# The relative bias of a banded attention: from reversing products on TensorE to a reversed key order and an add on VectorE

## The chip, the cores and the metric

One Trainium2 chip, one of its cores. The metric is the device time of one execution in microseconds (us). Lower is better. All matrices are float32; in the large projections each operand is split into two float32r parts (high and low), in the two attentions plain float32 products are used.

## The reference, cut to what matters

The reference is one transformer block with two attentions and 32 experts, and then two more blocks. Only the second attention of the first block is touched. It has 8 heads of 64, a sequence of 256, and a relative position bias:

```
q = q * 64**-0.5                                 # 8 heads, 256 positions, 64 columns
rel  = (kj - pad_len) - qi                       # key position less query position
bias = rel_bias[:, clip(rel, -128, 128) + 128]   # (8 heads, queries, keys)
s = einsum('bhqd,bhkd->bhqk', q, k) + bias
p = softmax(where(valid, s, -inf))               # whole chunks of 64 keys: not later than the query's chunk
o = einsum('bhqk,bhkd->bhqd', p, v)
```

With 256 positions no key lies further back than the band reaches, so the mask only hides the chunks of 64 keys that come after the query's own. The softmax is over all keys, so the order in which the keys stand in a row of scores does not matter to the sum and the maximum; the product with v needs them in the order of v.

## The kernel before, in words

The program is a sequence of phases. Each is a block in which the five engines run their own instruction lists and meet at its end. The first three are `phase_in`, `phase_attend` and `phase_merge`; then come the experts and the second block's phases.

`phase_in` projects the normed input into ten panels of 512 columns. SP loads weight chunks of 1 MB into a ring of four slots `raw`, ScalarE makes the high part `wh` (L156), VectorE the low part `wl` (L162), TensorE multiplies (L175 and L191), VectorE copies each finished panel out of PSUM (L489 to L497). Panels 3 and 4 are the queries and the keys of the second attention, `qkb`. Meanwhile GpSimd makes the tables: `ident`, then `rel_wide` (the bias of each head over 512 relative distances, clipped ends filled in), which it stores to DRAM as `rel_rows`. From there it loads `rel` by eight skewed transfers, one for each head (L430): partition p of a head gets the 384 numbers that start at p. It also makes `flip` (a 128x128 matrix with ones on the counter-diagonal), `mask` (0 or -1e30) and `alibi` (the first attention's bias with the mask added, L449 and L450).

In such a skewed table a row runs the wrong way: with the partition taken as the query, distance grows with the partition, while it should fall. The kernel puts that right by a product: `flip` (the counter-diagonal) turns the order of the partitions round, and the product is accumulated onto the scores in the same PSUM bank (L595).

`phase_attend` works through 16 units. A unit is one pair of heads (second attention) or one head with its two maps (first attention), and one tile of 128 queries. Units 0 to 7 are the first attention, 8 to 15 the second. TensorE's list in iteration u is written out by hand:

```
scores(u + 1)      # L592, two products of 64 rows; from unit 8 on each is followed by one of L595
mod_chunk(...)     # L301, one chunk of ada_w of the second block, 1 MB, straight from raw
mix(u - 2)         # L618 or L622, weights times v
flip(u - 1)        # L605, transposes of the weights
```

In iterations 0 to 3 a second `mod_chunk` follows. `scores(u)` waits for `biased` of unit u-2, `mix` for `keyed` and `kept`, `flip` for `weighed`. VectorE's list in iteration u is `bias(u)` (L707: scores plus `alibi` or `mask`, then the row maximum L710), `weigh(u - 1)` (L718 to L725: reciprocal of the row sum and the scaling of the weights `a`) and `keep(u - 2)` (L731). ScalarE does `exps(u)` (L656) and `key(u - 1)` (L665: the transposed weights out of PSUM). SP loads the `ada_w` chunks into the four slots of `raw` as `mod_chunk` frees them.

After the last unit VectorE normalises the first attention's output, TensorE transposes all of it, and the phase ends. `phase_merge` then multiplies with the branch weights and `w_out`, routes the tokens, and its SP list issues the first loads of expert weights, into buffers that lie over those of the attention. The experts' stage follows.

Of the kernel before, what the change touches and what calls it, by code (L numbers as in the profile page):

```python
# [14 lines left out]
P = 128  # L15
# [15 lines left out]
HB = 8  # L31
# [35 lines left out]
def make_mixing(c, ctx):  # L67

    c.qkb = c.sb("qkb", [P, 2, 4, S], ctx=ctx)
    c.va = c.sb("va", [P, TT, 512], ctx=ctx)  # L70
    c.vb = c.sb("vb", [P, TT, 512], ctx=ctx)
    c.mask = c.sb("mask", [P, TT, S], ctx=ctx)
    c.alibi = c.sb("alibi", [P, HA, TT, S], ctx=ctx)
    c.rel = c.sb("rel", [P, HB, 384], ctx=ctx)


def make_experts(c):


    with ExitStack() as early:  # L80
        make_mixing(c, early)
    left = c.sb("moe_left", [P, 2, BIG_CHUNK], ctx=c.moe)
    c.choice = c.sb("choice", [P, TT, 2, CAP], ctx=c.moe)
    c.slot_number = c.sb("slot_number", [P, SLOTS], ctx=c.moe)
    c.bias_in = c.sb("bias_in", [P, E * 16], ctx=c.moe)
    c.back = c.sb("back", [P, S], ctx=c.moe)
    make_routing(c)
    with ExitStack() as early:
        make_split(c, "1", early)
    halves = c.sb("moe_halves", [P, RING, BIG_CHUNK], ctx=c.moe)  # L90
    whole = c.raw[:, :, :, :].rearrange("p (s r) k n -> p s (r k n)", r=2)
    c.moe_ring = Stream(c, "moe_", [left[:, s] for s in range(2)] + [halves[:, s] for s in range(RING)]
                        + [whole[:, s] for s in range(RING // 2)])
    c.items = Items(c)
# [260 lines left out]
def phase_in(c):  # L355
# [4 lines left out]
    w_in = d["w_in"][0]  # L360
    c.qka = c.sb("qka", [P, 2, 4, S], ctx=c.mix)
    c.gates = c.sb("gates", [P, TT, 2 * D], ctx=c.mix)
    c.flip = c.sb("flip", [P, P], ctx=c.mix)
    c.at = c.sb("at", [P, 2, 512], ctx=c.mix)
    c.lam_in = c.at[:, 0, 0:4 * DA].rearrange("p (i j n) -> p i j n", i=2, j=2)
    c.subln = c.sb("subln", [P, 128], ctx=c.mix)
# [17 lines left out]
    with ExitStack() as local, nc.Block() as block:  # L384
        gain = c.sb("ln_in_gain", [P, D], ctx=local)
        shift = c.sb("ln_in_shift", [P, D], ctx=local)
        rel_wide = c.sb("rel_wide", [HB, 512], ctx=local)
        dist = c.sb("dist", [P, TT, S], ctx=local)
        away = c.sb("away", [P, TT, S], ctx=local)

# [16 lines left out]
        @block.gpsimd  # L407
        def _(pool):
            pool.memset(c.ident[:, :], 0.0).then_inc(ident_step, 1)
            pool.wait_ge(ident_step, 1)  # L410
            pool.affine_select(out=c.ident[:, :], in_=c.ident[:, :], compare_op=ALU.not_equal, fill=1.0, base=0,
                               pattern=[[-1, P]], channel_multiplier=1).then_inc(ident_step, 1)
            steps = 0

            def done(ins):
                nonlocal steps
                steps += 1
                ins.then_inc(pool_step, 1)
                pool.wait_ge(pool_step, steps)

            pool.wait_ge(bias_loaded, 16)
            lo, hi = S - 1 - CLIP, S - 1 + CLIP
            pool.tensor_copy(rel_wide[:, 0:lo], rel_wide[:, lo:lo + 1].to_broadcast([HB, lo]))
            done(pool.tensor_copy(rel_wide[:, hi + 1:512], rel_wide[:, hi:hi + 1].to_broadcast([HB, 511 - hi])))
            pool.dma_start(rel_rows, rel_wide[:, :]).then_inc(rel_stored, 16)
            pool.wait_ge(rel_stored, 16)
            for h in range(HB):
                pool.dma_start(c.rel[:, h, :], bass.AP(tensor=rel_rows.tensor, offset=h * 512, ap=[[1, P], [1, 384]])  # L430
                               ).then_inc(c.rel_loaded, 16)
            done(pool.memset(c.flip[:, :], 0.0))
            done(pool.affine_select(out=c.flip[:, :], in_=c.flip[:, :], compare_op=ALU.not_equal, fill=1.0,
                                    base=1 - P, pattern=[[1, P]], channel_multiplier=1))
            done(pool.memset(c.mask[:, :, :], 0.0))
            for m in range(TT):
                done(pool.memset(c.mask[0:CHUNK, m, m * P + CHUNK:S], NEG))
                if m < TT - 1:
                    done(pool.memset(c.mask[CHUNK:P, m, m * P + P:S], NEG))
            done(pool.iota(dist[:, :, :], pattern=[[P, TT], [-1, S]], base=0, channel_multiplier=1,  # L440
                           allow_small_or_imprecise_dtypes=True))
            done(pool.tensor_scalar(away[:, :, :], dist[:, :, :], -1.0, None, ALU.mult))

            for t, sign in ((dist, 1), (away, -1)):
                done(pool.affine_select(out=t[:, :, :], in_=t[:, :, :], compare_op=ALU.is_ge, fill=0.0, base=0,
                                        pattern=[[sign * P, TT], [-sign, S]], channel_multiplier=sign))
            done(pool.tensor_tensor(dist[:, :, :], dist[:, :, :], away[:, :, :], ALU.add))
            for h in range(HA):
                done(pool.tensor_scalar(away[:, :, :], dist[:, :, :], -2.0 ** (-8.0 * (h + 1) / HA), None, ALU.mult))  # L449
                done(pool.tensor_tensor(c.alibi[:, h], away[:, :, :], c.mask[:, :, :], ALU.add))  # L450
            pool.sem_inc(c.bias_ready, 1)

        @block.scalar
# [16 lines left out]
        @block.vector  # L470
        def _(dve):
            dve.wait_ge(x_loaded, 16 * TT)
            dve.wait_ge(norm_loaded, 32)
            layer_norm_dve(c, dve, 0, c.x, gain[:, :], shift[:, :])
            dve.sem_inc(normed, 1)
            for n in range(AHEAD):
                split_low(c, dve, W + n, n)
            turn_dve(c, dve, 0, c.bank)
            for p in range(panels):
                for n in range(2 * p + AHEAD, min(2 * p + AHEAD + 2, after)):  # L480
                    split_low(c, dve, W + n, n % RING)
                dve.wait_ge(c.used, W + 2 * p + 2)
                banks = c.bank[p % 2 * 2:p % 2 * 2 + 2]
                if p == 6:
                    dve.wait_ge(gate_loaded, 16)
                for b in range(2):
                    if kinds[p] == "T":

                        last = dve.tensor_scalar(outs[p][:, 2 * b:2 * b + 2, :],  # L489
                                                 banks[b][:, :].rearrange("p (k s) -> p k s", k=2),  # L490
                                                 SCALE if p in (0, 3) else 1.0, None, ALU.mult)
                    elif p < 6:
                        last = dve.tensor_copy(outs[p][:, b, :], banks[b][:, :])
                    else:
                        g = slice((p - 6) * COLS, (p - 5) * COLS)

                        last = dve.tensor_tensor(c.gates[:, b, g], banks[b][:, :], c.gates[:, TT - 1, g], ALU.add)  # L497
                        if b < TT - 1:
                            linked(c, dve, last)
                last.then_inc(evacuated, 1)  # L500
            dve.sem_inc(gates_ready, 1)
# [22 lines left out]
def phase_attend(c):  # L524
# [23 lines left out]
    with ExitStack() as local, nc.Block() as block:  # L548
# [34 lines left out]
        def _(pe):  # L583
            def scores(u):
# [4 lines left out]
                for j in range(2):  # L589
                    half = slice(j * 64, j * 64 + 64)  # L590
                    out = c.bank[2 * (u % 2) + j][:, 0:S]
                    mm = pe.matmul(out, qk[half, 0, h, m * P:m * P + P], qk[half, 1, h, :],  # L592
                                   start=True, stop=u < diff)
                    if u >= diff:
                        mm = pe.matmul(out, c.flip[:, :], c.rel[:, 2 * h + j, P - m * P:P - m * P + S],  # L595
                                       start=False, stop=True)
                mm.then_inc(scored, 1)

            def flip(u):
# [26 lines left out]
            scores(0)  # L626
            pe.wait_ge(silu_step, 2)
            for u in range(units + 2):
                if u + 1 == diff:
                    pe.wait_ge(c.rel_loaded, 16 * HB)  # L630
                if u + 1 < units:
                    scores(u + 1)
                mod_chunk(c, pe, part, u + min(u, EXTRA))
# [52 lines left out]
        def _(dve):  # L686
# [14 lines left out]
            def bias(u):  # L701
                h, m = u % diff // 2, u % 2
                dve.wait_ge(scored, u + 1)
                if u >= 2:
                    dve.wait_ge(weighed, u - 1)
                b = c.alibi[:, h, m] if u < diff else c.mask[:, m]
                dve.tensor_tensor(s[:, u % 2], c.psum[:, 2 * (u % 2):2 * (u % 2) + 2, 0:S],  # L707
                                  b.unsqueeze(1).to_broadcast([P, 2, S]), ALU.add).then_inc(biased, 1)
                dve.wait_ge(biased, u + 1)
                dve.tensor_reduce(nmax[:, u % 2, :], s[:, u % 2], AX, ALU.max, negate=True).then_inc(maxed, 1)  # L710

            def weigh(u):
# [9 lines left out]
                    dve.scalar_tensor_tensor(a[:, u % 2, 0], e[:, u % 2, 0], share[:, 0:1], a[:, u % 2, 1],  # L722
                                             ALU.mult, ALU.add).then_inc(weighed, 1)
                else:
                    dve.tensor_tensor(a[:, u % 2], e[:, u % 2], share[:, :].unsqueeze(2).to_broadcast([P, 2, S]),  # L725
                                      ALU.mult).then_inc(weighed, 1)

            def keep(u):
# [539 lines left out]
def phase_experts(c):  # L1268
# [9 lines left out]
    c.hid = c.sb("hid", [P, 2, COLS], ctx=c.exp)  # L1278
    c.y = c.sb("y", [P, COLS], ctx=c.exp)
    c.weighed = c.sb("weighed", [P, TT, SLOTS], ctx=c.exp)  # L1280
    c.acts = c.sb("acts", [P, KT, CAP], ctx=c.exp)
    c.gate_half = c.sb("gate_half", [P, 8, CAP], ctx=c.exp)
    c.up_half = c.sb("up_half", [P, 8, CAP], ctx=c.exp)
    c.sig = c.sb("sig", [P, 8, CAP], ctx=c.exp)
# [1264 lines left out]
```

## Time and profile before

| | us |
|---|---|
| median of 3 runs | 2092.8 (2089.57 to 2092.97) |
| profiled execution, its own time | 2093.78 |
| span of the profiled execution | 2092.0 |
| PE busy | 1839.9 (88%) |
| DVE busy | 788.3 (38%) |
| ACT busy | 489.4 (23%) |
| POOL busy | 50.0 (2%) |
| mean granted clock of TensorE | 0.945 of full |

The span is the time between the first and the last instruction that the profiler recorded. PE is TensorE's matmul, DVE is VectorE, ACT is ScalarE, POOL is GpSimd, SP is the engine that issues most loads. A float32 product appears as two matmul records. Durations of single matmuls overlap (they are pipelined), so that the work of a stretch of TensorE is read from the distance between starts, not from the sum of durations. The same holds, to a smaller degree, for VectorE. The second attention's units lie between about 176 and 220 us of the span.

### The profile page before, as it was taken

To read this page: it belongs to the slowest core of one execution; us is meant where nothing else is said; L and a number is where in the kernel's file an instruction comes from. 1 tells how busy PE (TensorE), PEld (TensorE's weight loads), DVE (VectorE), ACT (ScalarE), POOL (GpSimd) and SP (SyncE) were. 2 spreads that over 40 slices of the span, in tenths; PEclk is the share of its full clock that TensorE was granted. 3 is DMA by queue.
4 is the path that set the end of the run, shared out by engine and by line. 5 is a ranking of instruction groups with operands and counts; after the bars stand their busy time and mean duration, and the time that the engine had idled before them with its cause. 6 is when DMAs were issued, how large, how long until landed. Compare 5 with 4: busy or idle time off the path is not lost. (4 is left out here: it accounts for less than half of the span.)

```text
span 2092.0 us, 23989 instructions
## 1 busy us (share of the span) xinstructions
PE 1839.9 (88%) x9794; PEld 1132.5 (54%) x9795; DVE 788.3 (38%) x1024; ACT 489.4 (23%) x557; POOL 50.0 (2%) x74
## 2 busy tenths in 40 slices
PE   5999678999999898999999982978799979987998
PEld 5864454333333333333333321957688856566887
DVE  5545552221211221112211215556555555355544
ACT  3323421010100101010100002323243333234342
POOL 5000000000000000000000001010000000000000
PEclk9999888999999999999999996998899989788999
DMA  7548468999999999999999986544455523663651
GB/s 282 178 146 313 164 264 363 427 428 427 429 428 428 429 428 429 428 428 428 429 428 429 426 336 210 191 145 143 141 173 200 200 92 137 207 228 118 206 192 59
DMA packets 130798, 603.47 MB, mean 288 GB/s; under 512 B 12752, under 2 KB 12888, under 8 KB 106032
## 3 DMA queue, kind: packets, MB, share of 16 engines
q1 hardware_dynamic: 120096, 587.23, 70.9%
q10 hardware_dynamic: 10096, 13.77, 2.0%
q0 software_dynamic: 544, 1.59, 0.2%
q8 instruction: 45, 0.74, 0.1%
q14 instruction: 17, 0.14, 0.0%
HBM read 601.45 MB, written 1.11 MB: 288 GB/s over the span
## 5 line engine op out<-in xcount | busy, mean ns | idle before, releaser
L162 DVE TENSOR_TENSOR wl<-raw,wh 128x2048 fp32r<-128x2048 f32 x126 | 285.2, 2301 | 94.0 <-ACT wh L156 84.6
L156 ACT ACTIVATE wh<-raw 128x2048 fp32r<-128x2048 f32 x126 | 236.5, 1908 | 210.6 <-PE banks L175 124.8
L1156 PE MATMUL banks<-moe_halves,xs 128*64 128x512 f32 x1024 | 233.0, 603 | 12.0 <-DMA moe_halves<-in_w_exp_in 12.0
L191 PE MATMUL banks<-xth,wh 128*128 128x256 f32 x800 | 228.2, 285 | 11.0 <-DVE xtl L252 11.0
L191 PE MATMUL banks<-xtl,wh 128*128 128x256 f32 x800 | 228.2, 285 | 0.0
L191 PE MATMUL banks<-xth,wl 128*128 128x256 f32 x800 | 228.2, 285 | 0.0
L1205 DVE COPY hid<-banks 128x512 f32<-128x512 f32 x32 | 22.1, 692 | 523.0 <-PE banks L1156 523.0
L191 PEld LDWEIGHTS banks<-xth,wh 128*128 128x128 f32 x800 | 154.2, 193 | 12.9 <-DVE xtl L252 12.6
L1156 PEld LDWEIGHTS banks<-moe_halves,xs 128*64 128x64 f32 x1024 | 70.9, 138 | 159.8 <-issue 127.5
L175 PE MATMUL banks<-wh,xth 128*128 128x512 f32 x352 | 143.8, 409 | 13.3 <-PEq L548 5.9
L191 PEld LDWEIGHTS banks<-xtl,wh 128*128 128x128 f32 x800 | 153.3, 192 | 0.3
L191 PEld LDWEIGHTS banks<-xth,wl 128*128 128x128 f32 x800 | 153.0, 191 | 0.0
L175 PE MATMUL banks<-wl,xth 128*128 128x512 f32 x352 | 142.5, 405 | 0.0
L175 PE MATMUL banks<-wh,xtl 128*128 128x512 f32 x352 | 142.3, 404 | 0.0
L1156 PE MATMUL banks<-moe_left,xs 128*64 128x512 f32 x544 | 122.5, 597 | 6.0 <-DMA moe_left<-in_w_exp_in 5.9
L1168 PE MATMUL banks<-moe_halves,acts 128*64 128x512 f32 x512 | 114.7, 597 | 10.6 <-DMA moe_halves<-in_w_exp_out 10.6
L1156 PE MATMUL banks<-raw,xs 128*64 128x512 f32 x480 | 107.9, 596 | 4.5 <-DMA raw<-in_w_exp_in 4.5
L175 PE MATMUL banks<-wh,act_l 128*128 128x512 f32 x256 | 101.3, 396 | 0.0
L175 PE MATMUL banks<-wl,act_h 128*128 128x512 f32 x256 | 101.3, 396 | 0.0
L175 PE MATMUL banks<-wh,act_h 128*128 128x512 f32 x256 | 101.3, 396 | 0.0
L175 PEld LDWEIGHTS banks<-wh,xth 128*128 128x128 f32 x352 | 68.5, 195 | 32.3 <-issue 10.4
L1156 PEld LDWEIGHTS banks<-moe_left,xs 128*64 128x64 f32 x544 | 37.1, 137 | 83.2 <-issue 64.1
(342 smaller groups left out, 2052.1 us busy)
## 6 DMA issues: line engine op xcount, KB each, us to landing
moe_halves<-in_w_exp_in SPq DMA_DIRECT2D x64, 2048.0 KB, 34.7
moe_left<-in_w_exp_in SPq DMA_DIRECT2D x34, 2048.0 KB, 33.5
moe_halves<-in_w_exp_out SPq DMA_DIRECT2D x32, 2048.0 KB, 31.1
raw<-in_mlp_w SPq DMA_DIRECT2D x64, 1024.0 KB, 5.6
raw<-in_w_exp_in SPq DMA_DIRECT2D x30, 2048.0 KB, 34.7
raw<-in_ada_w SPq DMA_DIRECT2D x48, 1024.0 KB, 6.0
raw<-in_w_exp_out SPq DMA_DIRECT2D x18, 2048.0 KB, 31.1
moe_left<-in_w_exp_out SPq DMA_DIRECT2D x14, 2048.0 KB, 33.9
```

The lines of the kernel that those rows point to most:

```text
L156: act.activation(c.wh[:, slot], c.raw[:, slot], ACT.Copy).then_inc(c.high_ready, 1)
L162: dve.tensor_tensor(c.wl[:, slot], c.raw[:, slot], c.wh[:, slot].bitcast(F32), ALU.subtract).then_inc(c.low_ready, 1)
L175: mm = pe.matmul(banks[m][:, :], x[:, k0 + k, toks], w[:, slot, k], start=first and k == 0 and j == 0, stop=last and k == CK - 1 and j == ...
L191: mm = pe.matmul(out, w[:, slot, k, cols], x[:, k0 + k, :], start=first and k == 0 and j == 0 and b % 2 == 0, stop=last and k == CK - 1 an ...
L1156: mm = pe.matmul(c.bank[hid_banks(c, par) + pn][half * HALF:half * HALF + HALF, :], c.xs[:, 2 * k + r, own * CAP:own * CAP + CAP], st.slot ...
L1168: mm = pe.matmul(c.bank[hid_banks(c, par)][half * HALF:half * HALF + HALF, :], c.acts[:, 4 * j + r, :], st.slots[slot][:, at:at + COLS], s ...
L1205: dve.tensor_copy(c.hid[:, 1, :], c.bank[hid_banks(c, par) + 1]).then_inc(it.up_kept, 1)
```

## The change

The bias is laid out so that no turning is needed in TensorE. The stored rows are reversed (`rel_back`), and each head gets two skewed transfers of 256 numbers, one for each tile of queries, instead of one of 384. Along a row of the table the keys now run backwards. So the keys of the second attention are stored backwards too, by the copy out of PSUM of panel 4; the scores come out with reversed keys; and when VectorE scales the weights, it writes them with a negative step, so that they are in the usual order again for the transposes and the product with v. The mask, reversed, is added into `rel` by GpSimd, once. VectorE's add of unit 8 and later takes `rel` where it took `mask`. `flip` and the products L595 are gone. TensorE's wait for `rel_loaded` before unit 8 becomes a wait of VectorE for `bias_ready` at 2. `mask` lives in `phase_in` alone; `rel` grows from 384 to 512 numbers for each head; `acts` is allocated earlier, so that the tiles laid over the attention's buffers still cover them.

```diff
-    c.mask = c.sb("mask", [P, TT, S], ctx=ctx)
-    c.rel = c.sb("rel", [P, HB, 384], ctx=ctx)
+    c.rel = c.sb("rel", [P, HB, TT, S], ctx=ctx)
@@ make_experts / phase_experts
+    c.acts = c.sb("acts", [P, KT, CAP], ctx=c.moe)
-    c.acts = c.sb("acts", [P, KT, CAP], ctx=c.exp)
@@ phase_in, gpsimd
-            pool.dma_start(rel_rows, rel_wide[:, :]).then_inc(rel_stored, 16)
+            done(pool.tensor_copy(rel_back[:, 0:511], rel_wide[:, 510::-1]))
+            pool.dma_start(rel_rows[:, 0:511], rel_back[:, 0:511]).then_inc(rel_stored, 16)
             pool.wait_ge(rel_stored, 16)
             for h in range(HB):
-                pool.dma_start(c.rel[:, h, :], bass.AP(tensor=rel_rows.tensor, offset=h * 512, ap=[[1, P], [1, 384]])
-                               ).then_inc(c.rel_loaded, 16)
-            done(pool.memset(c.flip[:, :], 0.0))
-            done(pool.affine_select(out=c.flip[:, :], in_=c.flip[:, :], compare_op=ALU.not_equal, fill=1.0,
-                                    base=1 - P, pattern=[[1, P]], channel_multiplier=1))
+                for m in range(TT):
+                    pool.dma_start(c.rel[:, h, m, :], bass.AP(tensor=rel_rows.tensor, offset=h * 512 + m * P,
+                                                              ap=[[1, P], [1, S]])).then_inc(c.rel_loaded, 16)
...
             pool.sem_inc(c.bias_ready, 1)
+            pool.wait_ge(c.rel_loaded, 16 * HB * TT)
+            for h in range(HB):
+                done(pool.tensor_tensor(c.rel[:, h], c.rel[:, h], mask[:, :, ::-1], ALU.add))
+            pool.sem_inc(c.bias_ready, 1)
@@ phase_in, vector
-                        last = dve.tensor_scalar(outs[p][:, 2 * b:2 * b + 2, :],
+                        out = outs[p][:, 2 * b:2 * b + 2, ::-1] if p == 4 else outs[p][:, 2 * b:2 * b + 2, :]
+                        last = dve.tensor_scalar(out,
@@ phase_attend, tensor
                     mm = pe.matmul(out, qk[half, 0, h, m * P:m * P + P], qk[half, 1, h, :],
-                                   start=True, stop=u < diff)
-                    if u >= diff:
-                        mm = pe.matmul(out, c.flip[:, :], c.rel[:, 2 * h + j, P - m * P:P - m * P + S],
-                                       start=False, stop=True)
+                                   start=True, stop=True)
...
-                if u + 1 == diff:
-                    pe.wait_ge(c.rel_loaded, 16 * HB)
@@ phase_attend, vector
-                b = c.alibi[:, h, m] if u < diff else c.mask[:, m]
-                dve.tensor_tensor(s[:, u % 2], c.psum[:, 2 * (u % 2):2 * (u % 2) + 2, 0:S],
-                                  b.unsqueeze(1).to_broadcast([P, 2, S]), ALU.add).then_inc(biased, 1)
+                if u == diff:
+                    dve.wait_ge(c.bias_ready, 2)
+                b = (c.alibi[:, h, m].unsqueeze(1).to_broadcast([P, 2, S]) if u < diff
+                     else c.rel[:, 2 * h:2 * h + 2, m])
+                dve.tensor_tensor(s[:, u % 2], c.psum[:, 2 * (u % 2):2 * (u % 2) + 2, 0:S], b, ALU.add
+                                  ).then_inc(biased, 1)
...
-                    dve.tensor_tensor(a[:, u % 2], e[:, u % 2], share[:, :].unsqueeze(2).to_broadcast([P, 2, S]),
+                    dve.tensor_tensor(a[:, u % 2, :, ::-1], e[:, u % 2], share[:, :].unsqueeze(2).to_broadcast([P, 2, S]),
                                       ALU.mult).then_inc(weighed, 1)
```

## Rows read from the trace of the kernel before

**Rows 1.** Page: busy tenths of PE and of the DMA engines in 40 slices.

```profile
PE   5999678999999898999999982978799979987998
...
DMA  7548468999999999999999986544455523663651
```

**Rows 2.** Busy by stretch: stretch, length, PE, PEld, DVE, ACT, POOL, granted clock, DMA share, GB/s.

```profile
149.00:153.00 4.00, 4.00 (x20) 0.86 (x20) 3.46 (x10) 1.64 (x7) 0.00 (x0) 0.50 0.17 25
160.00:170.00 10.00, 7.13 (x52) 2.63 (x52) 3.74 (x12) 2.57 (x9) 0.00 (x0) 1.00 1.05 392
176.00:214.00 38.00, 38.00 (x208) 19.45 (x208) 19.09 (x45) 12.84 (x40) 0.00 (x0) 1.00 0.75 264
...
360.00:1200.00 840.00, 785.65 (x3824) 305.28 (x3820) 160.69 (x338) 88.14 (x145) 0.00 (x0) 1.00 1.01 428
```

**Rows 3.** Timeline of PE, one unit of the second attention: start, length, what.

```profile
204.13 0.69 PE L592 MATMUL banks<-qkb 64*128 64x256 f32 x2
204.76 0.70 PE L595 MATMUL banks<-rel,flip 128*128 128x256 f32 x2
...
206.64 1.07 PE L301 MATMUL banks<-raw,silu_c 128*32 128x512 f32 x8
207.64 1.11 PE L622 MATMUL banks<-vb,at 128*128 128x64 f32 x8
208.58 0.61 PE L605 MATMUL banks<-ident,a 128*128 128x128 f32 x4
209.12 0.70 PE L592 MATMUL banks<-qkb 64*128 64x256 f32 x2
```

**Rows 4.** Timeline of PE, first attention, and the second's first and last start.

```profile
148.01 1.23 PE L592 MATMUL banks<-qka 64*128 64x256 f32 x4 [2.05 <-DVE silu_c L689]
149.16 3.64 PE L301 MATMUL banks<-raw,silu_c 128*32 128x512 f32 x16
...
162.78 1.07 PE L301 MATMUL banks<-raw,silu_c 128*32 128x512 f32 x8 [1.01 <-DMA raw<-in_ada_w]
...
173.15 0.70 PE L592 MATMUL banks<-qka 64*128 64x256 f32 x4
173.78 1.06 PE L301 MATMUL banks<-raw,silu_c 128*32 128x512 f32 x8
...
175.86 0.70 PE L592 MATMUL banks<-qkb 64*128 64x256 f32 x2
...
214.11 1.06 PE L301 MATMUL banks<-raw,silu_c 128*32 128x512 f32 x8
```

**Rows 5.** Timeline of DVE, one iteration in the second attention.

```profile
208.78 0.29 DVE L731 COPY o<-banks 128x128 f32<-128x128 f32 x1 [2.58 <-PE banks L622]
208.99 0.68 DVE L707 TENSOR_TENSOR s<-banks,mask 128x512 f32<-128x512 f32 x1
209.71 0.69 DVE L710 TENSOR_REDUCE nmax<-s 128x2 f32<-128x512 f32 x1
210.31 0.15 DVE L718 RECIPROCAL share<-total 128x2 f32<-128x2 f32 x1
210.50 0.69 DVE L725 TENSOR_TENSOR a<-s,share 128x512 f32<-128x512 f32 x1
```

**Rows 6.** Timeline of POOL in the first phase.

```profile
22.10 4.28 POOL L430 DMA_DIRECT2D rel<-rel_rows  x8 [6.91 <-DMA rel_rows<-rel_wide]
...
43.24 1.31 POOL L450 TENSOR_TENSOR alibi<-away,mask 128x512 f32<-128x512 f32 x1
...
48.14 2.35 POOL L450 TENSOR_TENSOR alibi<-away,mask 128x512 f32<-128x512 f32 x1
```

**Rows 7.** Timeline of DVE in the first phase.

```profile
43.60 5.72 DVE L162 TENSOR_TENSOR wl<-raw,wh 128x2048 fp32r<-128x2048 f32 x2
...
54.91 4.48 DVE L162 TENSOR_TENSOR wl<-raw,wh 128x2048 fp32r<-128x2048 f32 x2
64.90 1.29 DVE L493 COPY va<-banks 128x512 f32<-128x512 f32 x2 [5.51 <-PE banks L175]
```

More of the change, by code:

```diff
@@ L362, in phase_in @@
     c.gates = c.sb("gates", [P, TT, 2 * D], ctx=c.mix)
-    c.flip = c.sb("flip", [P, P], ctx=c.mix)
     c.at = c.sb("at", [P, 2, 512], ctx=c.mix)
@@ L386, in phase_in @@
         shift = c.sb("ln_in_shift", [P, D], ctx=local)
-        rel_wide = c.sb("rel_wide", [HB, 512], ctx=local)
+        mask = c.sb("mask", [P, TT, S], ctx=local)
+        rel_wide = c.at[0:HB, 1, :]
+        rel_back = c.sb("rel_back", [HB, 512], ctx=local)
         dist = c.sb("dist", [P, TT, S], ctx=local)
@@ L426, in _ @@
             done(pool.tensor_copy(rel_wide[:, hi + 1:512], rel_wide[:, hi:hi + 1].to_broadcast([HB, 511 - hi])))
-            pool.dma_start(rel_rows, rel_wide[:, :]).then_inc(rel_stored, 16)
+            done(pool.tensor_copy(rel_back[:, 0:511], rel_wide[:, 510::-1]))
+            pool.dma_start(rel_rows[:, 0:511], rel_back[:, 0:511]).then_inc(rel_stored, 16)
             pool.wait_ge(rel_stored, 16)
             for h in range(HB):
-                pool.dma_start(c.rel[:, h, :], bass.AP(tensor=rel_rows.tensor, offset=h * 512, ap=[[1, P], [1, 384]])
-                               ).then_inc(c.rel_loaded, 16)
-            done(pool.memset(c.flip[:, :], 0.0))
-            done(pool.affine_select(out=c.flip[:, :], in_=c.flip[:, :], compare_op=ALU.not_equal, fill=1.0,
-                                    base=1 - P, pattern=[[1, P]], channel_multiplier=1))
-            done(pool.memset(c.mask[:, :, :], 0.0))
+                for m in range(TT):
+                    pool.dma_start(c.rel[:, h, m, :], bass.AP(tensor=rel_rows.tensor, offset=h * 512 + m * P,
+                                                              ap=[[1, P], [1, S]])).then_inc(c.rel_loaded, 16)
+            done(pool.memset(mask[:, :, :], 0.0))
             for m in range(TT):
-                done(pool.memset(c.mask[0:CHUNK, m, m * P + CHUNK:S], NEG))
+                done(pool.memset(mask[0:CHUNK, m, m * P + CHUNK:S], NEG))
                 if m < TT - 1:
-                    done(pool.memset(c.mask[CHUNK:P, m, m * P + P:S], NEG))
+                    done(pool.memset(mask[CHUNK:P, m, m * P + P:S], NEG))
             done(pool.iota(dist[:, :, :], pattern=[[P, TT], [-1, S]], base=0, channel_multiplier=1,
@@ L449, in _ @@
                 done(pool.tensor_scalar(away[:, :, :], dist[:, :, :], -2.0 ** (-8.0 * (h + 1) / HA), None, ALU.mult))
-                done(pool.tensor_tensor(c.alibi[:, h], away[:, :, :], c.mask[:, :, :], ALU.add))
+                done(pool.tensor_tensor(c.alibi[:, h], away[:, :, :], mask[:, :, :], ALU.add))
+            pool.sem_inc(c.bias_ready, 1)
+            pool.wait_ge(c.rel_loaded, 16 * HB * TT)
+            for h in range(HB):
+                done(pool.tensor_tensor(c.rel[:, h], c.rel[:, h], mask[:, :, ::-1], ALU.add))
             pool.sem_inc(c.bias_ready, 1)
```

## The prediction

> **What bounds the kernel now.** I read the page first. TensorE is busy in 9 tenths of most slices, and in the middle of the span the DMA engines are too [rows 1]. The busy time by stretch then says which stage has which limit. Between 360 and 1200 us, the experts, the DMA share is 1.01 at 428 GB/s [rows 2]: that stage goes at the pace of the loads. The changed stretch, 176 to 214 us, is another sort: TensorE is busy in all of its 38.00 us at a granted clock of 1.00, VectorE in 19.09, ScalarE in 12.84, and the loads use 0.75 of the DMA engines [rows 2]. There TensorE's own list is the limit.
>
> The timeline of TensorE shows the list without a gap: one unit of the second attention takes from 204.13 to 209.12, which is 4.99 us [rows 3]. It splits, by starts, into 206.64 - 204.13 = 2.51 us of scores and bias products, 1.00 of the ada_w chunk, 0.94 of `mix` and 0.54 of transposes. VectorE waits 2.58 us for `mix` in each of these units [rows 5]. So what TensorE loses from its list comes off the unit, until another chain is the slowest.
>
> Does a gain at 214 us reach the end? What follows (the last units, the norm, the transposes, the merge) is a chain that starts with the last unit's weights; the experts' loads are issued by SP inside the merge, behind its barrier and its products. So the load-bound stage starts earlier by what the attention saves, and nothing in it has a start of its own. I take the shift to be carried whole.
>
> **The products that go.** Each unit has two pairs of records of L595. By the starts the first takes 204.76 to about 205.39, and the four pairs of L592 and L595 together take the 2.51 us: 0.63 each [rows 3]. Removing two pairs gives 1.26 us for each unit, eight units: 10.0 us.
>
> **What the removed products kept apart.** This is the term that the diff does not show. The two score products of a unit use 64 rows each, one the lower half of the array's rows, the other the upper. In the first attention they follow each other directly, and all four records together take 173.15 to 173.78, 0.63 us [rows 4]. In the second attention, with a product of 128 rows between them, two records alone take 0.63 us [rows 3]. Same shapes, same clock (1.00), half the time for each. So next to each other the halves run at the same time, and apart they don't. After the change they stand next to each other in the second attention too: another 0.63 us for each unit. The scores fall from 2.51 to 0.63, by 1.88 us. The Trainium skill, TensorEngine Tiling (Array Packing), Key Properties, says that tiles of the array work independently and that a change of the tiling mode drains the array; the trace agrees, with 0.63 us for four records against 0.63 us for two.
>
> **The unit after.** TensorE: 4.99 - 1.88 = 3.11 us. Is anything else slower? VectorE: its iteration takes, by starts, 0.72 (L707), 0.60 (L710), 0.19 (L718), 0.69 (L725) and 0.21 (L731), that is 2.41 us [rows 5]. The chain across engines: `keep` and so the whole iteration of VectorE starts when `mix` ends (208.78, at 209.12 - 0.34), and the weights are ready at 211.19, 2.07 us after the unit's start. `flip` needs them at 0.63 + 1.00 + 0.94 = 2.57 us after the start. Slack 0.50 us. ScalarE has 12.84 us of work in 38.00, about 1.7 for each unit of 4.99 [rows 2], and fits in 3.11 with room. The chunk loads: at 392 GB/s a chunk of 1.049 MB takes 2.68 us, and at that pace the first attention already waits for them (1.01 us before the chunk at 162.78) [rows 2, 4]. A unit of 3.11 us is above 2.68, though by little.
>
> The first units of the stretch are different, because `mix` and the transposes are still those of the first attention. From 175.86 to 214.11 there are eight iterations, 38.25 us [rows 4]; five at 4.99 are 24.95, so the first three are 13.30, 4.43 each. Less 1.88 that is 2.55 us, under the pace of the loads of 2.68. I put 2.7 for each.
>
> Sum: 38.25 before, 3 x 2.7 + 5 x 3.11 = 23.65 after, 14.6 us less. After 214.11 no scores are left, and the tail is as it was.
>
> **VectorE's operands.** The add L707 has the same size, with `rel` in place of a broadcast `mask`: 0.68 us as before; the alibi and the mask form have that shape. The scaling L725 writes with a step of minus one. No row shows such a write. Below: no gain is possible from an order, so 0.69 us. Above: twice that, 1.38 us, by which VectorE would be at half its rate. I take 0.69, since the engine goes one element after another (512 numbers in 0.69 us) and the order only changes the address. At 1.38 the weights come at 2.76 against 2.57: `flip` is late by 0.19 us and more through the chain's next turn, 0.1 to 0.3 for a unit, and 0.7 for the last one, in which nothing hides it: about 2 us in all, a saving of 12.6. The copy of panel 4 writes backwards too; before the copy of a panel VectorE sits idle 5.51 us [rows 7], so even twice 1.29 us is hidden.
>
> **GpSimd's work.** It gains one reversed copy over 8 partitions, eight more transfers to issue (4.28 us for eight [rows 6]) and eight adds of 128x512, each 1.31 to 2.35 us, as the alibi adds [rows 6]; it loses the two operations on `flip`. The alibi adds now end at 48.14 + 2.35 = 50.5 us; afterwards at 50.5 + 4.3 plus a little, and the eight adds 10.5 to 18.8 us later: 65 to 75 us. They are first wanted at about 178 us: over 100 us of cover. The transfers bring 16 x 128 rows of 1 KB, 2.10 MB, instead of 8 x 128 rows of 1.5 KB, 1.57 MB; at 392 GB/s [rows 2] the difference is 1.3 us of the DMA engines, and a ring of four chunks covers that for the projections. Cost: nothing. Without that cover it would be VectorE's unit 8 that waits, and TensorE behind it.
>
> What the adds may disturb is VectorE's splitting. It did before: two splits took 5.72 us while GpSimd worked on the tables, and 4.48 us when it did not [rows 7]. That is 1.24 us of a reserve of 5.51 for each panel; 15 to 25 us of new GpSimd work touch two or three panels. Even a delay of 4.5 us, a doubling, would be hidden. The Trainium skill, SBUF — State Buffer, Who interferes with whom, says that a VectorE instruction with two SBUF inputs contends with a GpSimd instruction that reads SBUF, and that the second to issue waits for the whole of the other; the trace agrees with a loss (1.24 us), and by that rule too the sum stays as it is.
>
> **The sum against the run.** The profiled execution took 2093.78 with a span of 2092.0. Span after: 2092.0 - 14.6 = 2077.4, its time 2079.2. The median before was 2092.8, 1 us under the profiled one: predicted median 2078.2, 0.70% less. No change that a measurement of this kernel can tell is one within 0.2%, 4.2 us.
>
> **Rivals.**
>
> A, the forecast: 14.6 us, 2078.2. Chance 0.70.
>
> B, only the reversing products' own time goes: the score halves stay one after the other for a reason of the second attention's own. 10.0 us, 2082.8. For it: the halves of `qkb` have never been seen next to each other. Against: the forms of the records are the same as of `qka`, and the 0.63 us for four records holds there. 0.09.
>
> C, VectorE becomes the slowest: the negative step costs up to double. 12.6 us, 2080.2; with the add slower too, less. For: slack of only 0.50 us. Against: nothing in the rows; it is unknown rather than indicated. 0.11.
>
> D, the other side: TensorE's clock falls in the second attention, because its list is no longer gapless. At the lower of the two levels (granted 0.50 between 149 and 153 us, 1.2 GHz against 2.4) the four records of L592 took 148.01 to 149.16, 1.15 us, instead of 0.63: 1.83 times [rows 2, 4]. Then five units of 3.11 x 1.83 = 5.7 and three of 4.7 make 42.6 us, 4.3 over the present 38.25, and the last units' 2.5 us grow by 2: slower by 6.3, 2099.1. It decides from the point where over two thirds of the stretch is at the lower level. Against: between 160 and 170 us TensorE is busy 7.13 of 10 us, with gaps of 1 us, and is granted 1.00 [rows 2]; the new stretch is nearly gapless. 0.03.
>
> E, the change does not do what it says in time: `rel` with the mask is late at unit 8. It would need to be ready only after 178 us to cost anything, and after 193 us to eat all; with 65 to 75 us that takes adds of 14 us each instead of 1.31 to 2.35. Time 2092.8 at 193 us. 0.01.
>
> F, the gain is given back later: a stage after the attention has a limit of its own, or the clock rises later after the pauses of the tail. Nothing in the rows has such a start; a rest for the unknown. Within 4.2 us of before: about 2090. 0.06.
>
> **How the numbers follow.** A alone: the three first units may take 2.5 to 3.1 and the others 3.1 to 3.3, and medians before spread over 3.4 us, so 2075.0 to 2081.5. B and C add the upper part: range 2074.8 to 2084.0, which leaves D, E, F and half of the tails out. Faster by over 0.2%: A, B, C, 0.90, and a little of F, 0.91. Same 0.05, slower 0.04.
>
> **What the profile after should show.** In the second attention four records of L592 in 0.63 us, directly followed by L301; no row of L595 (its number shifts) with `flip`; starts of units 3.1 us apart; VectorE idle before `keep` 0.7 us instead of 2.58; L725 at 0.69 us; DMA share near 0.9 to 1.0 in the stretch; `phase_merge` starting at 227 instead of 241.6 us; the experts' stage of the same length. Two records in 0.63 us would show B; L725 over 0.69 us C; a granted clock under 1.00 between 176 and 205 us D. I would be wrong above all if the halves don't overlap, or if the chunk loads, at 2.68 us a piece, are slower there.

## The result

| | kernel before | changed kernel |
|---|---|---|
| median | 2092.39 us (6 runs) | 2075.59 us (6 runs) |
| profiled execution, its own time | 2093.78 | 2076.02 |
| span | 2092.0 | 2074.2 |

The ratio of the two is 0.9912, with a 95% interval of 0.9887 to 0.9937: 18.4 us faster, where 14.6 was forecast. The ratio applied to the first median, 2092.8, gives 2074.4, just under the range's low end of 2074.8. The direction, the place and the mechanism in the attention held; a term was missing, and it lies 1000 us after the place of the change.

One execution weighs on this ratio. Five of the six of the changed kernel took 2074.38 to 2077.65 us, the sixth 2062.65, and it alone has a mean granted clock of 0.955 where the five have 0.942 to 0.946. Without it the averages are 2092.23 and 2076.01 us, a ratio of 0.9922 and 16.2 us, which is 2076.6 on the first median and inside the range. The last experiments below show what such an execution may be.

The timeline of TensorE in the changed kernel shows the stretch that the forecast was about, with its first three iterations, one later unit and the end:

```profile
175.68 0.70 PE L598 MATMUL banks<-qkb 64*128 64x256 f32 x4
176.31 1.06 PE L301 MATMUL banks<-raw,silu_c 128*32 128x512 f32 x8
...
178.56 0.70 PE L598 MATMUL banks<-qkb 64*128 64x256 f32 x4
...
181.26 0.70 PE L598 MATMUL banks<-qkb 64*128 64x256 f32 x4
183.12 1.06 PE L301 MATMUL banks<-raw,silu_c 128*32 128x512 f32 x8 [1.15 <-DMA raw<-in_ada_w]
...
194.52 0.70 PE L598 MATMUL banks<-qkb 64*128 64x256 f32 x4
195.15 1.07 PE L301 MATMUL banks<-raw,silu_c 128*32 128x512 f32 x8
196.14 1.10 PE L625 MATMUL banks<-vb,at 128*128 128x64 f32 x8
197.09 0.61 PE L608 MATMUL banks<-ident,a 128*128 128x128 f32 x4
197.62 0.70 PE L598 MATMUL banks<-qkb 64*128 64x256 f32 x4
...
200.73 1.06 PE L301 MATMUL banks<-raw,silu_c 128*32 128x512 f32 x8
```

All four score records of a unit now fit in 0.63 us (175.68 to 176.31), as in the first attention [rows 4], and a unit takes 3.10 us (194.52 to 197.62) instead of 4.99 [rows 3]. The stretch from 175.68 to 200.73 takes 25.05 us instead of 38.25 [rows 4]: 13.2 us less.

VectorE's timeline in the same unit answers to [rows 5]:

```profile
194.18 0.29 DVE L735 COPY o<-banks 128x128 f32<-128x128 f32 x1 [0.70 <-PE banks L625]
194.39 0.68 DVE L711 TENSOR_TENSOR s<-banks,rel 128x512 f32<-128x512 f32 x1
195.10 0.69 DVE L714 TENSOR_REDUCE nmax<-s 128x2 f32<-128x512 f32 x1
195.71 0.15 DVE L722 RECIPROCAL share<-total 128x2 f32<-128x2 f32 x1
195.90 0.69 DVE L729 TENSOR_TENSOR a<-s,share 128x512 f32<-128x512 f32 x1
```

The write with a negative step takes 0.69 us, the same as forwards; the wait for `mix` fell from 2.58 to 0.70.

Busy time by stretch in the changed kernel (columns as in [rows 2]):

```profile
176.00:201.00 25.00, 23.67 (x180) 12.44 (x180) 19.18 (x45) 12.82 (x41) 0.00 (x0) 1.00 1.05 386
...
360.00:1200.00 840.00, 785.91 (x3822) 306.11 (x3820) 162.57 (x338) 88.50 (x145) 0.00 (x0) 0.99 1.01 428
```

The granted clock stayed at 1.00, so rival D did not come. But the DMA share in the attention is now 1.05: the loads are as full there as TensorE.

GpSimd and VectorE in the first phase, where the tables are made:

```profile
21.93 8.49 POOL L434 DMA_DIRECT2D rel<-rel_rows  x16 [6.17 <-DMA rel_rows<-rel_back]
...
51.68 14.90 POOL L455 TENSOR_TENSOR rel<-rel,mask 128x512 f32<-128x512 f32 x8 [0.18 <-POOL alibi L451]
```

```profile
54.39 5.57 DVE L162 TENSOR_TENSOR wl<-raw,wh 128x2048 fp32r<-128x2048 f32 x2
64.39 1.29 DVE L499 COPY va<-banks 128x512 f32<-128x512 f32 x2 [4.42 <-PE banks L175]
```

The adds end at 66.6 us, 110 us before they are wanted. While they run VectorE loses 1.1 us in a panel (5.57 against 4.48) and its idle time falls from 5.51 to 4.42 [rows 7]: hidden, as forecast.

**Where the rest came from.** Subtracting the times of the same events in the two traces gives the gain as it stood at each:

| event | before | after | difference |
|---|---|---|---|
| first scores of the second attention | 175.86 | 175.68 | -0.2 |
| first chunk product after the last scores | 214.11 | 200.73 | -13.4 |
| first product of the merge | 241.62 | 228.60 | -13.0 |
| first load issued in the experts' phase | 336.96 | 322.71 | -14.3 |
| last product of the experts | 1254.73 | 1240.56 | -14.2 |
| VectorE's first instruction of the next phase | 1264.94 | 1244.81 | -20.1 |
| start of the norm behind it | 1271.70 | 1253.76 | -17.9 |
| span | 2092.0 | 2074.2 | -17.8 |

The attention's gain is carried through the load-bound stage. The 1.3 us that come on top in the merge go with the granted clock: between its first product and the first load of the experts' phase it is 0.85 on average before and 0.90 after, and TensorE is busy 77.1 against 75.6 us for the same 350 matmuls. From 28 to 38 us into the merge the clock is 0.50 before, and 0.72 and then 1.00 after.

Then 6.0 us more appear between two instructions, of which 2.2 are given back at the next wait. Here is that place in both kernels, before and after, first TensorE's last product of the experts and then VectorE:

```profile
1254.73 1.99 PE L1191 MATMUL banks<-y,back 64*128 64x512 f32 x8 [0.69 <-ACT y L1216]
```

```profile
1264.94 2.35 DVE L1593 SCALAR_TENSOR_TENSOR x<-x,banks 128x1024 f32<-128x1024 f32 x2 [20.61 <-PEq L1454]
1271.70 2.47 DVE L215 BATCH_NORM_STATS2 stats<-x 128x6 f32<-128x512 f32 x4 [4.40 <-DMA ln<-in_ln_b]
```

```profile
1240.56 1.99 PE L1195 MATMUL banks<-y,back 64*128 64x512 f32 x8 [0.69 <-ACT y L1220]
```

```profile
1244.81 2.35 DVE L1596 SCALAR_TENSOR_TENSOR x<-x,banks 128x1024 f32<-128x1024 f32 x2 [14.51 <-PEq L1457]
1253.76 2.47 DVE L215 BATCH_NORM_STATS2 stats<-x 128x6 f32<-128x512 f32 x4 [6.60 <-DMA ln<-in_ln_b]
```

This is the dead time: from the end of the product to VectorE's start it is 8.22 us before (1256.72 to 1264.94) and 2.26 us after (1242.55 to 1244.81). No engine does anything in between. What lies there in the program is `phase_spill`: code for tokens over an expert's capacity, a long body of TensorE's instructions, that is skipped by a branch when there are none. The releaser that the row names is TensorE's sequencer (PEq) at that phase.

### The profile page after: what moved, and what is told of

Read it like the earlier page. It is cut to its first block and busy times, and to the rows that moved or that the text cites. A ratio compares the mean times of both kernels' runs of the same rounds, so it can differ in the third digit from the quotient of the medians.

```text
span 2074.2 us, 23939 instructions
## 1 busy us (share of the span) xinstructions
PE 1827.8 (88%) x9762; PEld 1124.7 (54%) x9763; DVE 789.5 (38%) x1024; ACT 489.5 (24%) x557; POOL 66.1 (3%) x89
## 5 line engine op out<-in xcount | busy, mean ns | idle before, releaser
L175 PE MATMUL banks<-wh,xth 128*128 128x512 f32 x352 | 143.2, 407 | 14.3 <-PEq L554 5.9
```

Of the source, the lines that this page charges most:

```text
L175: mm = pe.matmul(banks[m][:, :], x[:, k0 + k, toks], w[:, slot, k], start=first and k == 0 and j == 0, stop=last and k == CK - 1 and j == ...
```

## The experiments

**The place of the code behind the skip.** The change takes 32 matmul and 32 weight-load instructions out of TensorE's program, and a wait. Everything behind moves forward in the program by that much. Two kernels put that to the test, one in each direction, by waits on a count that has long been reached. The expectations reckon 130 waits as 64 instructions and 382 as 192, and pieces of 16 KB; no run measures this reckoning by itself. Two further kernels look for the edge.

```diff
 # e1_pad_after, on the changed kernel; e6 with 80, e7 with 116
+            for _ in range(130):
+                pe.wait_ge(silu_step, 2)
             pe.wait_ge(c.mixer_turned, 1)
             turn_pe(c, pe, 4, o, c.bank)
```

> The changed kernel with TensorE's program made as long again as before: 130 waits on a count that has long been reached, in the list after the last unit, where TensorE is idle for over 9 us. Everything behind them then lies in the program where it lay before. Theory L (where the code lies): the dead time between the last product of the experts and VectorE's first instruction of the next phase, 8.2 us before and 2.3 us after the change, comes from fetching instructions past the skipped spill phase, and depends on where that code lies. Expected: the dead time is 8.2 us again, the span about 3.8 us above the 2074.2 of the changed kernel, 2078.0. Theory T (timing): the dead time changed because the attention ended earlier against the loads, or by chance: it stays at 2.3 us, the span at 2074 to 2075.

```diff
 # e2_pad_before, on the kernel before
+            for _ in range(382):
+                pe.wait_ge(ident_step, 2)
             pe.wait_ge(ident_step, 2)
             pe.wait_ge(normed, 1)
```

> The kernel before with 382 such waits at the start of TensorE's list, where it waits 17.9 us for the norm. The code behind lies in the program as it does in the changed kernel, if the fetches come in pieces of 16 KB: 64 instructions less or 192 more is the same place in a piece. Theory L: dead time 2.3 instead of 8.2 us, span about 3.8 us under 2092.0, 2088.2, and a small gain against the kernel before with nothing of the change in it. Theory T: dead time 8.2 us, span 2092.

> The changed kernel with 80 waits in the idle stretch of TensorE instead of the 130 that brought the 8.2 us of dead time back. Theory L: there is one edge in the place of the code, and this length stays on the near side: dead time 2.3 us, span 2074. Rival: the dead time grows with the length of the program: 8.2 - 2.3 = 5.9 us for 130 waits, so 5.9 us here.

> The same with 116 waits. Theory L: beyond the edge, dead time 8.2 us and span 2078. Rival, growing with length: 7.6 us.

Dead time is from the end of the last product to VectorE's start, as above:

| kernel | last product ends | VectorE starts | dead time | span |
|---|---|---|---|---|
| before | 1256.72 | 1264.94 | 8.2 | 2092.0 |
| before, 382 waits (e2) | 1258.04 | 1260.30 | 2.3 | 2089.6 |
| changed | 1242.55 | 1244.81 | 2.3 | 2074.2 |
| changed, 80 waits (e6) | 1243.97 | 1246.22 | 2.3 | 2076.1 |
| changed, 116 waits (e7) | 1243.40 | 1251.60 | 8.2 | 2082.4 |
| changed, 130 waits (e1) | 1241.50 | 1249.66 | 8.2 | 2078.7 |

There are two values and an edge between 80 and 116 waits, not a slope, and the waits are 1000 us away from the place where they cost. e6 and e7 were run once each, but two kernels made for other ends, below, fit: e3 adds 8 products and has 2.3 us, e5 adds 16 and has 8.2. Neither the number of instructions in itself nor the time at which the attention ends decides, since e2 is long and late and has 2.3 us, and e1 and e7 are early and have 8.2. It is where the code lies.

That also shows that 3.8 us of the gain of the two traces are no merit of the change. e1 has all of the change but the place: a median of 2078.55 us, ratio 0.9925 (0.9899 to 0.9951). Two of its eight executions are again of the quick sort, 2064.43 and 2066.78; the other six are 13.0 us under the kernel before on average (its own quick one of 2079.05 left out likewise), where the changed kernel was 16.2 under it. So the change without its luck is worth 13 us, 1.6 less than the forecast.

e2 has nothing of the change and a median of 2090.0, ratio 0.9996 (0.9982 to 1.001). By its trace the waits at its start delay the attention by 1 us, and the skip gives back more; in the timed runs the sum can't be told from no change, where 3.8 us had been expected. The spans of e6 and e7 are 2 and 4 us above what was expected. The merge took 1.6 and 1.4 us longer than in the changed kernel, at the lower mean clock of 0.85 again, and in e7 the stretch from the norm behind the skip to the third attention took 2.6 us more (499.35 against 496.79), on which no experiment was made.

What the dead time is spent on is indicated by the DMA queue of instructions, taken over just the dead time, first in the kernel before, then in e1, then in the changed kernel over its own 2.2 us:

```profile
DMA packets 1248, 2.47 MB, mean 301 GB/s; under 512 B 48, under 2 KB 48, under 8 KB 1247
...
q8 instruction: 1, 0.02, 0.8%
```

```profile
DMA packets 1239, 2.45 MB, mean 299 GB/s; under 512 B 48, under 2 KB 48, under 8 KB 1238
...
q8 instruction: 1, 0.02, 0.8%
```

```profile
DMA packets 431, 0.85 MB, mean 386 GB/s; under 512 B 16, under 2 KB 16, under 8 KB 431
```

Where the dead time is long, one transfer of 0.02 MB of instructions lies in it; where it is short there is none. It lies at 1261 to 1262 us in the kernel before, at 1246 to 1247 in e1, at 1248 to 1249 in e7 and at 1262 to 1263 in e5, each time about 3 us before VectorE starts. In the changed kernel and in e2 the next such transfer comes only after VectorE's start. That fits a branch whose target is not yet there when the skip is taken, and a piece of code that must be fetched while the DMA engines are still full of weight loads. The trace does not show TensorE's sequencer waiting for this transfer, so the fetch is the likely cause and the place of the code the shown one.

**The score halves.**

```diff
 # e3_small_product_between, on the changed kernel, after each unit's first score product
+                    if u >= diff and j == 0:
+                        pe.matmul(c.bank[2 * (u % 2)][:, S:S + 16], c.ident[:, :], c.ident[:, 0:16],
+                                  start=True, stop=True)
```

> The changed kernel with one small product of 128 rows by 16 columns between the two score products of each unit of the second attention, into a part of the bank that nobody reads. Theory K (kept apart): the two halves of 64 rows run at the same time only if nothing of 128 rows stands between. Expected: two records of the score line take about 0.63 us again, the scores of a unit 0.63 + 0.63 and about 0.1 for the small one, so a unit takes 3.8 us instead of 3.11, and the stretch of eight units about 5 us more (the first units have 1.15 us of waiting for a load to give). Rival: the halves overlap whatever is between; only the small product's own 0.1 us is added, a unit of 3.2 us, the stretch under 1 us longer.

The timeline of TensorE in e3, one unit (the product put between is L601):

```profile
190.14 0.70 PE L598 MATMUL banks<-qkb 64*128 64x256 f32 x2
190.76 0.40 PE L601 MATMUL banks<-ident 128*128 128x16 f32 x2
191.09 0.70 PE L598 MATMUL banks<-qkb 64*128 64x256 f32 x2
191.72 1.07 PE L301 MATMUL banks<-raw,silu_c 128*32 128x512 f32 x8
...
194.19 0.70 PE L598 MATMUL banks<-qkb 64*128 64x256 f32 x2
```

Each half takes 0.63 us by itself again, and the unit 4.05 us instead of 3.10. Of the 0.95, 0.63 is the lost overlap and 0.32 (190.76 to 191.09) the small product, three times what I had put for it. The median was 2083.3 us, ratio 0.9959 (0.9945 to 0.9973). The stretch took 30.78 us (175.57 to 206.35) instead of 25.05, 5.7 us more where about 5 was expected. So the overlap is real and worth 0.63 us for a unit, and one product of 16 columns between is enough to lose it.

**The change with the products put back, and the products gone without the change.**

```diff
 # e5_products_kept, on the changed kernel, after each score product
+                    if u >= diff:
+                        mm = pe.matmul(c.bank[2 * (u % 2) + j][:, S:2 * S], c.ident[:, :], c.vb[:, 0, 0:S],
+                                       start=True, stop=True)
```

> The changed kernel with two idle products of 128 rows by 256 columns in each unit of the second attention, after each score product, into halves of the banks that nobody reads: TensorE's list is as before, all else is the change. Theory: the gain is all in TensorE's list and the place of its code. Expected: units of 4.99 us, dead time at the spill 8.2 us, span 2091 to 2093. Rival: the tables, the reversed order or the folded mask save or cost something by themselves: a span under 2089 or over 2095.

The timed runs had a median of 2092.99 us against 2091.47 of the kernel before, ratio 1.0004 (0.9995 to 1.0014): with TensorE's list kept, the tables, the reversed keys, the folded mask and the other place of the tiles together can't be told from nothing, within 1 us of gain and 3 us of cost. The dead time was 8.2 us. The profiled execution itself took 2082.87 us, 10 us under the median of its kernel; that is the last group below.

```diff
 # e4_products_only, on the kernel before
                     mm = pe.matmul(out, qk[half, 0, h, m * P:m * P + P], qk[half, 1, h, :],
-                                   start=True, stop=u < diff)
-                    if u >= diff:
-                        mm = pe.matmul(out, c.flip[:, :], c.rel[:, 2 * h + j, P - m * P:P - m * P + S],
-                                       start=False, stop=True)
+                                   start=True, stop=True)
```

> The kernel before without the products by flip, and nothing else changed: it leaves out the relative bias. Theory: all of the gain lies in TensorE's list and in the place of its code, none in the tables, the reversed order or the move of the mask. Expected: units of 3.11 us, the stretch 25 us instead of 38.25, dead time at the spill 2.3 us, span about 2074. Rival: GpSimd's longer work or the reversed writes cost something that this kernel does not pay: span under 2073.

Its stretch took 173.71 to 198.43, 24.7 us, as expected. Its time, 2258.95 us, says nothing about the change, and its dead time can't be read: from the experts' last product to VectorE's next instruction it is 189 us (1241.35 to 1430.70), where the others have 2.3 or 8.2. Without the bias the tokens are routed otherwise, an expert is over its capacity, and the spill phase that all the others skip is run. A kernel that leaves something out of the data can be read by stage only.

**The loads in the attention.**

```diff
 # e8_fewer_loads, on the changed kernel
-FIRST_MOD = 10
+FIRST_MOD = 8
...
             for j in range(part.chunks):
+                if j == RING:
+                    for n in range(2):
+                        expert(n)
                 n = part.W + j
                 load_chunk(c, sp, n, n % RING, ada_source(c, 0, FIRST_MOD * PANEL + j), j >= RING)
-            for n in range(2):
-                expert(n)
```

> The changed kernel with 16 instead of 20 chunks of ada_w in the attention (none twice in an iteration), the four others with the merge's, and the first two loads of expert weights issued ahead of these. Theory P (pace of the loads): the 1.15 us that TensorE still waited for a load in the second attention, and the waits in the first, come from the backlog of the doubled chunks. Expected: no wait for raw in the second attention, its eight units 23.7 us instead of 25.05, and the whole attention 4 to 6 us shorter; in the merge TensorE waits for the four chunks that are moved there, up to 7 us, so that the span is between 2069 and 2078. Rival: the wait comes from the loads' own latency in each slot and stays at 1 us.

The eight units took 168.01 to 191.86, 23.85 us, with no wait for `raw`. So 1.2 of the 1.4 us by which the stretch of the changed kernel (25.05) exceeds the forecast (23.65) are the backlog of the loads; of the 0.2 left, 0.17 is a wait for VectorE's weights in the first iteration. The attention was even 8.9 us shorter up to the merge (219.72 against 228.60), where 4 to 6 had been expected. But the first load of the experts' phase was issued at 322.37 against 322.71, and the median was 2075.71, that of the changed kernel. All but 0.3 of the 8.9 us went: the chunks only moved, and TensorE waited 5.9 us for them in the merge. So a shorter attention is carried to the end when work is removed from it, as in the change, and not when it is put off.

**The clock 560 us later.** The profiled execution of e5 was 10 us shorter than the median of its kernel. It reaches the third attention when the kernel before does (1768.45 against 1768.20 us), and all of the difference lies behind. In both, the clock falls to 0.50 about 3 us after the start of that attention. In e5 it is back at 1.00 3 us later, in the kernel before only after some 30 us (1771 to 1802). TensorE stands idle for 1.10 us at the barrier before it.

```diff
 # e9_fill_gap, on the changed kernel, at the end of TensorE's list in the phase before
+            pe.wait_ge(evacuated, 5)
+            for _ in range(4):
+                pe.matmul(c.bank[0][:, :], c.xth[:, 0, 0:P], c.xth[:, 0:2, :].rearrange("p k s -> p (k s)"),
+                          start=True, stop=True)
 # e10_fill_gap_and_start, besides, in iterations 0, 1 and 2 of the third attention
+                for _ in range((6, 4, 4)[u] if u < 3 else 0):
+                    pe.matmul(c.bank[6][:, :], ...)
```

> The changed kernel with four products of 128x512, whose result nobody reads, in the 1.1 us in which TensorE waits at the barrier before the third attention, 560 us after the place of the change. One execution of an earlier experiment, 12 us under the others, had the granted clock at 1.00 in that attention, where all others show 0.50 for some 27 us from 3 us after that gap on. Theory G (the gap drops the clock): with the gap filled the clock stays at 1.00, span about 12 us less, 2062. Rival: the clock falls because of the small products that follow, and filling the gap does nothing: 2074.

> The same, and 14 more such products in the first three iterations of that attention, 3.3 us of work. Theory S (the small products at its start drop the clock): now the clock stays at 1.00, 12 us less and 3.3 us more, span 2065. If the four in the gap are enough, this is 3 us slower than e9; if neither helps, 2077.

> The changed kernel once more, as the measure for the other two on the same chip: 2074 to 2077 by median, dead time at the spill 2.3 us.

The gap and the stage behind it, in the changed kernel again (e11), TensorE's timeline and the busy time by stretch:

```profile
1747.23 1.91 PE L2312 MATMUL banks<-ident,qk 128*128 128x128 f32 x16
1750.23 0.46 PE L2368 MATMUL banks<-kt,qt 64*128 64x128 f32 x2 [1.10 <-PEq L2219]
```

```profile
1750.00:1756.00 6.00, 5.77 (x24) 2.77 (x24) 1.43 (x4) 3.03 (x5) 0.53 (x1) 0.77 0.01 3
1756.00:1780.00 24.00, 24.00 (x80) 12.45 (x76) 6.59 (x14) 3.44 (x9) 0.00 (x0) 0.50 0.54 175
```

And in e9:

```profile
1749.34 1.18 PE L2318 MATMUL banks<-xth 128*128 128x512 f32 x4
1750.81 0.46 PE L2372 MATMUL banks<-kt,qt 64*128 64x128 f32 x2 [0.30 <-PEq L2219]
```

```profile
1750.00:1756.00 6.00, 5.70 (x30) 2.95 (x28) 1.40 (x4) 3.40 (x6) 0.53 (x1) 1.00 0.02 3
1756.00:1780.00 24.00, 24.00 (x147) 13.57 (x146) 10.62 (x23) 7.09 (x18) 0.00 (x0) 1.00 0.84 268
```

With four products in the gap the clock stays at its upper level, and 147 instead of 80 matmuls are done in the same 24 us. The median of e9 is 2062.33 us, against 2074.82 of the changed kernel on the same chip: 12.5 us less. Ratio to the kernel before 0.986 (0.9829 to 0.9891). e10 has 2065.09, the 3 us of its further products above, and e9 is the fastest kernel of this study.

That the gap makes the clock fall is not shown by this. e10 fills the gap in the same way, and its clock fell all the same, from about 1753.2 to 1756.5 us, and rose while the further products ran:

```profile
1753.50:1754.00 0.50, 0.50 (x2) 0.00 (x0) 0.47 (x2) 0.00 (x0) 0.00 (x0) 0.50 0.00 0
1754.00:1756.00 2.00, 2.00 (x7) 1.67 (x7) 0.03 (x2) 1.09 (x2) 0.00 (x0) 0.50 0.00 0
1757.00:1758.00 1.00, 1.00 (x10) 0.16 (x9) 0.95 (x2) 0.00 (x0) 0.00 (x0) 1.00 0.00 0
```

In the traces what separates a quick execution from the others is that the lower level does not last: none in e9, 3 us in e10 and in e5, 30 us in the changed kernel and the one before.

The times of single executions say how often. Of the eight of e9 and e10 seven were quick, and one of e9 took 2072.44 us. Without the filling 4 of 57 were quick over the changed kernel, e1 to e3, e5 to e8 and e11 (2062.65, 2064.43, 2066.78 and 2082.87), and 2 of the 52 of the kernel before (2079.05 and 2077.64); those six had a mean granted clock of 0.950 to 0.955. So the filling shifts the odds clearly, and what decides in a single execution stays open.

## Why the prediction was right and where it was wrong

**Right.** The products removed and the overlap returned: scores 2.51 to 0.63 us. The unit: 3.11 forecast, 3.10 measured. What was costed at nothing can't be told from nothing (e5). VectorE kept a slack, and the negative step was free, so C fell; B fell by e3 and by the changed kernel's own rows; D by the granted clock of 1.00; E by adds that ended at 66.6 us.

**The step that failed** is "So the load-bound stage starts earlier by what the attention saves, and nothing in it has a start of its own. I take the shift to be carried whole." Up to the experts' last product it held: 13.2 us at the attention, 14.2 there. But I looked only at waits for data and at the stage's pace. I did not count that the removed instructions shift TensorE's code, and that 8.2 us of dead time at the skipped phase were there to be lost or won by it. It was to be seen before: VectorE's wait for PEq at that barrier, with no engine working. As a term: 6.0 us at the skip, 2.2 given back at the wait for `ln_b`, net 3.8. F named a later place only for giving the gain back; the term had the other sign.

**What luck did.** The place of the code is luck: 116 waits more in the same list bring the old dead time back (e7). The one quick execution of 2062.65 us is luck too, and the forecast had no term for the clock of the third attention. Together they carry the time out of the range, and without either it lies inside: 18.4 less 3.8 is 14.6, and 16.2 without that execution.

**The mis-sized term.** 14.6 us for the stretch, 13.2 measured. The rows of the pace of the loads were right (2.68 us a chunk), but I used the pace as a floor for each of the first three iterations, and did not add up the backlog: the third took 3.93 us (181.26 to 185.19), with 1.15 of waiting for a load. e8 shows it, at 23.85 us without the backlog against 23.65 forecast.

About 1 us more came between the merge's start and the experts' phase (13.0 to 14.3). This part varies by as much between the kernels of the study, and its mean granted clock with it: 94.1 us in the changed kernel and 93.9 in e1 at 0.90, 95.3 in the kernel before and 95.7 in e6 at 0.85. The forecast had no term for this clock, and no experiment was made on it.

Net: 13.2 at the attention, 1.0 in the merge, 3.8 at the skip, less 0.2 in the rest, makes the 17.8 us of the two spans.

## What to carry to other kernels

Products on different row halves of the array overlapped here only as neighbours in the list: look at the distance between starts for the pair, and ask of every instruction between two such products what it keeps apart as well as what it costs. Before costing a removal on an engine with a long program, look for dead times at skipped code and barriers, where no engine works: they can change by several us with the place of the code, so check by padding the program before crediting a change with them. A few idle products in a short gap of TensorE are worth a try where the stage behind it shows the lower clock. And look at every single time, not only at the ratio: one quick execution in six moved this one by 2 us.

## What the runs showed of the hardware that was not expected

- A dead time of either 2.3 or 8.2 us at a branch over skipped code, by the code's place alone, with one instruction transfer in the long one, about 3 us before its end.
- A stage of small products behind a gap of 1.10 us ran some 30 us at a granted clock of 0.50, although TensorE was busy throughout. With four products in the gap the median was 12.5 us less; the clock stayed at 1.00 in one trace (e9), and in another (e10) it fell even so and was back after 3 us.
- A product of 128 rows by 16 columns between products of 64 rows took 0.32 us, besides the 0.63 us of lost overlap.
